# A loop over four experts, six of eleven weight positions and one token operand buffer in a mixture-of-experts kernel

## What is computed

```
g_idx = argmax(x @ w_group + b_group)                   # one group of 8
top_val, top_idx = top_k(expert logits of that group, 2)  # 2 of its 8 experts
h = silu(xb @ w_gate[e]) * (xb @ w_up[e])               # e = 0..63, width 512
y += gate * (h @ w_down[e])
```

## Time and profile before

| what | us |
|---|---|
| median of three executions | 1652.43 |
| the profiled execution: span from first to last instruction | 1650.3 |
| PE busy | 1344.0 |
| ACT busy | 442.9 |
| DVE busy | 539.8 |
| stage of the experts' weights, DMA at full rate, about | 740 to 1637 |

### The profile page before, as it was taken

The page is one execution under the profiler, slowest core; times in us unless marked ns, Lnnn a source line. Parts: engine busy times, 40 slices in busy tenths (PEclk is TensorE's granted clock), DMA queues, the critical chain, the costliest instruction groups (busy, mean ns, idle before and its releaser), DMA issues.

```text
span 1650.3 us, 30064 instructions
## 1 busy us (share of the span) xinstructions
PE 1344.0 (81%) x12966; PEld 1011.0 (61%) x12966; DVE 539.8 (33%) x908; ACT 442.9 (27%) x752; POOL 61.1 (4%) x83
## 2 busy tenths in 40 slices
PE   8999999999999999999667676667667666667655
PEld 8989999878999998876333343343334343334332
DVE  6666555766555578541000000000000000000001
ACT  5354433644433356421111011011011011101101
POOL 3000000001000025000000000000000000000000
PEclk9999999999999999999988987898798798998797
DMA  9545453533555544389999999999999999999996
GB/s 348 193 174 179 177 203 124 180 117 120 201 189 178 179 149 174 153 356 428 428 427 425 428 427 427 426 427 428 427 426 427 427 427 427 427 428 426 427 427 251
DMA packets 45842, 520.37 MB, mean 315 GB/s; under 512 B 5535, under 2 KB 5796, under 8 KB 8228
## 3 DMA queue, kind: packets, MB, share of 16 engines
q1 hardware_dynamic: 44496, 517.12, 76.9%
q0 software_dynamic: 1040, 1.52, 0.4%
q10 hardware_dynamic: 196, 0.08, 0.0%
HBM read 517.65 MB, written 1.05 MB: 314 GB/s over the span
## 4 chain that ended last, share of the span: by engine, by line
DMA 48%; PE 45%; DVE 4%; ACT 2%; issue 1%; POOL 0%; DVEq 0%; SPq 0%; ACTq 0%
DMA ring<-in_moe_units 28%; DMA x_slots<-in_moe_units 14%; PE ps L265 11%; PE ps L267 11%; PE ps L266 11%; DMA work<-in_moe_units 6%; PE ps L2057 4%; PE ps L2066 2%; DVE w_split L230 1%; PE ps L2080 1%; PE ps L2100 1%; PE ps L272 1%; DVE xT_lo L512 1%; ACT w_split L226 0%; PE ps L942 0%
## 5 line engine op out<-in xcount | busy, mean ns | idle before, releaser
L265 PE MATMUL ps<-xT_hi,w_split 128*128 128x256 f32 x960 | 269.7, 281 | 1.8 <-DVE xT_lo L512 1.8
L230 DVE TENSOR_TENSOR w_split<-ring,w_split 128x2048 fp32r<-128x2048 f32 (+2 forms) x105 | 237.2, 2261 | 97.6 <-ACT w_split L226 96.4
L267 PE MATMUL ps<-xT_hi,w_split 128*128 128x256 f32 x960 | 268.2, 279 | 0.0
L266 PE MATMUL ps<-xT_lo,w_split 128*128 128x256 f32 x960 | 268.1, 279 | 0.0
L2258 DVE TENSOR_TENSOR work<-ps,work 128x128 f32<-128x128 f32 x64 | 18.7, 292 | 755.4 <-ACT work L2183 755.4
L2057 PE MATMUL ps<-ring,work 128*32 128x256 f32 x2464 | 182.5, 447 | 95.3 <-DMA ring<-in_moe_units 95.2
L226 ACT ACTIVATE w_split<-ring 128x2048 fp32r<-128x2048 f32 (+2 forms) x109 | 203.7, 1871 | 153.0 <-PE ps L267 153.0
L2057 PEld LDWEIGHTS ps<-ring,work 128*32 128x32 f32 x2464 | 84.6, 124 | 185.3 <-DMA ring<-in_moe_units 101.5
L265 PEld LDWEIGHTS ps<-xT_hi,w_split 128*128 128x128 f32 x960 | 180.2, 188 | 4.0 <-issue 2.9
L266 PEld LDWEIGHTS ps<-xT_lo,w_split 128*128 128x128 f32 x960 | 179.9, 187 | 0.9
L267 PEld LDWEIGHTS ps<-xT_hi,w_split 128*128 128x128 f32 x960 | 180.4, 188 | 0.0
(11 more groups left out here) (341 smaller groups left out, 1665.5 us busy)
## 6 DMA issues: line engine op xcount, KB each, us to landing
ring<-in_moe_units SPq DMA_DIRECT2D x114, 2048.0 KB, 46.7
work<-in_moe_units SPq DMA_DIRECT2D x38, 2048.0 KB, 46.6
x_slots<-in_moe_units SPq DMA_DIRECT2D x38, 2048.0 KB, 46.6
ring<-in_ffn_units SPq DMA_DIRECT2D x66, 1024.0 KB, 4.8
ring<-in_conv_units SPq DMA_DIRECT2D x15, 1024.0 KB, 11.4
ring<-in_win_units SPq DMA_DIRECT2D x9, 1024.0 KB, 4.8
ring<-in_wo_units SPq DMA_DIRECT2D x4, 1024.0 KB, 5.5
ring<-in_wout_units SPq DMA_DIRECT2D x4, 1024.0 KB, 4.8
```

The lines of the kernel that those rows point to most:

```text
L230: dve.tensor_tensor(w_split[:, u % SPLIT, 1, 0:n], raw[:, u % RAW, 0:n], w_split[:, u % SPLIT, 0, 0:n].bitcast(F32), ALU.subtract).then_in ...
L265: pe.matmul(out_ap, stat_hi, mov_hi, start=first, stop=False, skip_group_check=True)
L266: pe.matmul(out_ap, stat_hi, mov_lo, start=False, stop=False, skip_group_check=True)
L267: return pe.matmul(out_ap, stat_lo, mov_hi, start=False, stop=last, skip_group_check=True)
```

## The change

The loop body holds 4 steps in place of 20 and is run 13 times; steps 1 to 9 are written out ahead of it. `kept_slot` becomes an ordinary position, so there are eleven. Doubles 0 to 28 go round all eleven; from double 29 on (`RING_FROM`) the stream goes round six of them (places 7, 8, 9, 10, 0, 1: five pieces of `ring` and one of `x_slots`). SP's loop body holds six doubles and is run 26 times; its issues ahead of that are written out. A double waits for the reading of the one eleven earlier in the first part, six earlier from double 35 on. The token operand has one buffer. ACT therefore writes its first half in the step of lane 3, between `turned` and `gu_out`, in place of lane 2, after `gu_out`.

```diff
-    xstat = [wk(XSTAT + 1024 * b, 1024).rearrange("p (k m) -> p k m", m=P) for b in range(3)]
+    xstat = wk(XSTAT, 1024).rearrange("p (k m) -> p k m", m=P)
...
-    FIRST_STEP, LOOP = 2, 20
-    LOOPS = (NE - FIRST_STEP) // LOOP
+    FIRST_STEP, LOOP = 10, 4
+    LOOPS = (NE - 2 - FIRST_STEP) // LOOP
...
-    SLOTS = 10
+    SLOTS = 11
+    KEPT = 4
     LOOP_DOUBLES = 3 * LOOP
-    KEPT = 4
+    RING_FROM, IN_RING = 3 * FIRST_STEP - 1, 6
...
     def place(d):
 
-        return (d if d < KEPT else d - 1) % SLOTS
+        if d >= RING_FROM:
+            d = RING_FROM + (d - RING_FROM) % IN_RING
+        return d % SLOTS
+
+    def last_in(d):
+
+        return d - (IN_RING if d >= RING_FROM + IN_RING else SLOTS)
...
+        def refill(r, d):
+            sp.wait_ge(s("moe_read"), r * DOUBLES + last_in(d) + 1)
+            whole(d, d)
...
-            for k in range(SLOTS):
-                sp.wait_ge(s("moe_read"), r * DOUBLES + (k + 1 if k < KEPT else k + 2))
-                whole(SLOTS + k + 1, SLOTS + k + 1)
-            with sp.Fori(2, (DOUBLES - 1) // SLOTS) as i:
-                for k in range(SLOTS):
-                    sp.wait_ge(s("moe_read"), r * DOUBLES + i * SLOTS + (k - SLOTS + 2))
-                    whole(SLOTS + k + 1, i * SLOTS + (k + 1))
-            sp.wait_ge(s("moe_read"), r * DOUBLES + (DOUBLES - 1 - SLOTS + 1))
+            for d in range(SLOTS, RING_FROM + IN_RING):
+                refill(r, d)
+            first = RING_FROM + IN_RING
+            with sp.Fori(0, (DOUBLES - 1 - first) // IN_RING) as i:
+                for k in range(IN_RING):
+                    sp.wait_ge(s("moe_read"), r * DOUBLES + i * IN_RING + (last_in(first + k) + 1))
+                    whole(first + k, i * IN_RING + (first + k))
+            sp.wait_ge(s("moe_read"), r * DOUBLES + last_in(DOUBLES - 1) + 1)
...
             turned(E - 1, 1 - par, T_BANK)
+            if more and lane == 3:
+                x_half(quad + 1)
             gu_out(at, d, par)
-            if more and lane == 2:
-                x_half(quad + 1, x_buffer(q // QUAD + 1))
             y_out(at, d + 2, 1 - par, T_BANK)
...
-            one_step(step, r, 1, True)
+            for e in range(1, FIRST_STEP):
+                one_step(step, r, e, True)
```

More of the change, by code:

```diff
@@ L1938, in program @@
     QUADS = NE // QUAD
-    FIRST_STEP, LOOP = 2, 20
-    LOOPS = (NE - FIRST_STEP) // LOOP
+    FIRST_STEP, LOOP = 10, 4
+    LOOPS = (NE - 2 - FIRST_STEP) // LOOP
     DOUBLES = 3 * NE
-    SLOTS = 10
+    SLOTS = 11
+    KEPT = 4
     LOOP_DOUBLES = 3 * LOOP
-    KEPT = 4
-    assert KEPT < 3 * FIRST_STEP - 1
+    RING_FROM, IN_RING = 3 * FIRST_STEP - 1, 6
+    assert LOOPS * LOOP + FIRST_STEP == NE - 2 and LOOP == QUAD
+    assert LOOP_DOUBLES % IN_RING == 0 and RING_FROM > 2 * SLOTS
     def place(d):
-        return (d if d < KEPT else d - 1) % SLOTS
-    assert LOOP_DOUBLES % SLOTS == 0 and LOOP % QUAD == 0 and LOOP // QUAD == 5
-    assert LOOPS * LOOP + FIRST_STEP == NE - 2
+        if d >= RING_FROM:
[3 more added lines that the diff above has]
+        return d - (IN_RING if d >= RING_FROM + IN_RING else SLOTS)
     def expert_loop(eng, r, step):
@@ L1965, in one_step @@
         step(e, r * NE + e, r * QUADS + e // QUAD, e - i * LOOP, more, (r, i))
-    def x_buffer(quad):
-        return xstat[(0, 1, 0, 1, 2)[quad % 5]]
     def slot_of(d):
-        if d == KEPT:
+        if place(d) == KEPT:
             return kept_slot[:, :, :]
-        k = place(d)
+        k = place(d) - (place(d) > KEPT)
         if k in (0, 1, 5):
@@ L1992, in turn_of @@
         k = place(d)
-        return r * len(range(k, DOUBLES - 1, SLOTS)) + i * (LOOP_DOUBLES // SLOTS) + ((d if d < KEPT else d - 1) // SLOTS + 1)
+        every = sum(place(x) == k for x in range(DOUBLES))
+        ringed = k in [place(RING_FROM + x) for x in range(IN_RING)]
+        return r * every + (i * (LOOP_DOUBLES // IN_RING) if ringed else 0) + sum(place(x) == k for x in range(d + 1))
     def doubles_before(at, d):
@@ L2012, in whole @@
         def whole(d, at):
-            sp.dma_start(slot_of(d), a["moe_units"][bass.ds(at, 1)].rearrange("a p (u n) -> p (a u) n", u=2))\
-                .then_inc(s("moe_kept") if d == KEPT else landed(d), 16)
+            sp.dma_start(slot_of(d), a["moe_units"][bass.ds(at, 1)].rearrange("a p (u n) -> p (a u) n", u=2)).then_inc(landed(d), 16)
+        def refill(r, d):
+            sp.wait_ge(s("moe_read"), r * DOUBLES + last_in(d) + 1)
+            whole(d, d)
         def one_round(r):
@@ L2018, in one_round @@
                 sp.wait_ge(s("combined"), r + 1)
-            if isinstance(r, int):
+                for d in range(SLOTS):
+                    whole(d, d)
+            else:
                 whole(KEPT, KEPT)
-            for k in range(SLOTS):
-                if isinstance(r, int):
+                for k in range(SLOTS - 1):
                     first_free(k)
-                whole(k if k < KEPT else k + 1, k if k < KEPT else k + 1)
-            for k in range(SLOTS):
-                sp.wait_ge(s("moe_read"), r * DOUBLES + (k + 1 if k < KEPT else k + 2))
-                whole(SLOTS + k + 1, SLOTS + k + 1)
-            with sp.Fori(2, (DOUBLES - 1) // SLOTS) as i:
-                for k in range(SLOTS):
-                    sp.wait_ge(s("moe_read"), r * DOUBLES + i * SLOTS + (k - SLOTS + 2))
-                    whole(SLOTS + k + 1, i * SLOTS + (k + 1))
-            sp.wait_ge(s("moe_read"), r * DOUBLES + (DOUBLES - 1 - SLOTS + 1))
+                    d = k + (k >= KEPT)
+                    whole(d, d)
+            for d in range(SLOTS, RING_FROM + IN_RING):
[6 more added lines that the diff above has]
+            sp.wait_ge(s("moe_read"), r * DOUBLES + last_in(DOUBLES - 1) + 1)
             for half, sem in ((0, landed(DOUBLES - 1)), (1, s("moe_last"))):
@@ L2045, in double, with up_like @@
         def double(at, d):
[L2046 to L2049, removed]
+            pe.wait_ge(landed(d), turn_of(at, d) * 16)
             return slot_of(d)
-        def up_like(at, d, b, x, lane, half):
+        def up_like(at, d, b, lane, half):
             w = double(at, d).rearrange("p u (k s c) -> p (u k) s c", k=2, s=2)
@@ L2056, in up_like @@
                 for j in range(QUAD):
-                    last = pe.matmul(ps[CAP * j:CAP * j + CAP, b, 0:BLK], x[:, 4 * half + k, CAP * lane:CAP * lane + CAP],
+                    last = pe.matmul(ps[CAP * j:CAP * j + CAP, b, 0:BLK], xstat[:, 4 * half + k, CAP * lane:CAP * lane + CAP],
                                      w[:, k, j // 2, BLK * (j % 2):BLK * (j % 2) + BLK], start=half == k == 0, stop=half == 1 and k == 3,
@@ L2106, in step @@
             d, par, lane = 3 * q - 1, q % 2, q % QUAD
-            x = x_buffer(q // QUAD)
             if lane == 0:
                 pe.wait_ge(s("xa"), quad + 1)
-            up_like(at, d, par, x, lane, 0)
+            up_like(at, d, par, lane, 0)
             pe.wait_ge(s("y_out"), E)
             turn(E - 1, 1 - par, T_BANK)
-            if q >= FIRST_STEP:
+            if q >= 2:
                 combine(par)
@@ L2116, in step @@
                 pe.wait_ge(s("xd"), quad + 1)
-            up_like(at, d + 1, par, x, lane, 1)
+            up_like(at, d + 1, par, lane, 1)
             if more and lane >= 2:
@@ L2129, in one_round @@
             pe.wait_ge(s("xa"), quad + 1)
-            up_like((r, 0), 0, 0, xstat[0], 0, 0)
+            up_like((r, 0), 0, 0, 0, 0)
             pe.wait_ge(s("xd"), quad + 1)
-            up_like((r, 0), 1, 0, xstat[0], 0, 1)
-            one_step(step, r, 1, True)
+            up_like((r, 0), 1, 0, 0, 1)
+            for e in range(1, FIRST_STEP):
+                one_step(step, r, e, True)
             expert_loop(pe, r, step)
@@ L2141, in one_round @@
             d = 3 * q - 1
-            x = x_buffer(q // QUAD)
-            up_like(at, d, 1, x, QUAD - 1, 0)
+            up_like(at, d, 1, QUAD - 1, 0)
             pe.wait_ge(s("y_out"), g + (NE - 1))
@@ L2146, in one_round @@
             combine(1)
-            up_like(at, d + 1, 1, x, QUAD - 1, 1)
+            up_like(at, d + 1, 1, QUAD - 1, 1)
             pe.wait_ge(s("a_mul"), g + (NE - 1))
@@ L2167, in moe_act, with x_half @@
         act.sem_inc(s("y_out"), 1)
-        def x_half(quad, buf):
+        def x_half(quad):
             act.wait_ge(s("x_first"), quad + 1)
             for k in range(4):
-                last = act.activation(buf[:, k, :], bank(X_BANK, P, P * k), ACT.Copy, scale=col("norm2", k))
+                last = act.activation(xstat[:, k, :], bank(X_BANK, P, P * k), ACT.Copy, scale=col("norm2", k))
             last.then_inc(s("xa"), 1)
@@ L2200, in one_round @@
             g = r * NE
-            x_half(r * QUADS, xstat[0])
+            x_half(r * QUADS)
             gu_out((r, 0), 0, 0)
-            one_step(step, r, 1, True)
+            for e in range(1, FIRST_STEP):
+                one_step(step, r, e, True)
             expert_loop(act, r, step)
```

(8 more changed lines are left out.)

## The result

The changed kernel takes 1642.07 us (median of four, 1640.07 to 1646.30), the kernel before 1653.56 us (four, 1652.24 to 1656.77). The ratio is 0.993, interval 0.9913 to 0.9947: faster by 0.7%, 11.5 us. The prediction said no change, 1652.4, and the time lies outside its range.

A forecast was written before the change was run, and what follows sets the result against it. The weights' DMA stream was taken to bound the kernel: 737.2 + 901.0 + 12.1 = 1650.3 us span, all changes 0, plus 2.1 to the median gave 1652.4 us, range 1648.5 to 1658.

The forecast's parts named there:

- What bounds the kernel: Experts' stage: it lasts as long as its bytes take, 4.89 us a double at 427 GB/s, PE busy 68%.
- Start of the stream: First refill: eleven positions are filled ahead in both kernels and it still waits for double 0's reading; effect 0.
- Six positions in place of ten: DMA queue from double 35 on: issue to landing falls to 27.1 us in the median, 15.6 us slack left; cost 0.
- The bound of 2 us for another rate: Stream with the shorter queue: same rate taken; 427 against 428 GB/s, 0.2%, gives 2 us on either side.
- Ten more turns: Loop jumps of PE, ACT and DVE, 12 for 2: PE catches up after each; cost 0, 49 us if uncovered.
- Rival (a): PE's 12 jumps: fetch stalls add up beyond 15.6 us and idle DMA, giving 1676 to 1701 us; chance 0.03.
- The fetches' use of the DMA engines: Instruction packets in the stream, priced by bytes at 427 GB/s: 0 taken, ends -1.5 and +0.9 us.
- The rest of the sum: Stream from first refill to last landing: some 13 us of 901 in doubles longer than 4.89 us, cause not read.
- Rival (c): Stream: the 13 us of longer doubles hang on positions or long queues and go, down to 1640 us; chance 0.05.
- One token operand: ACT's first half in lane 3: written 1.2 to 2.5 us before PE comes to its wait; cost 0.
- The tail: ACT's idle time before the closing squares, with a jump over a shorter copy: up to 1.2 us shorter or unchanged; taken 0.

The follow-up runs named there:

- the run with 9000 increments: The changed kernel with 9000 semaphore increments, which nothing waits for, on idle GpSimd during the experts' stage: 1689.33 us, ratio 1.0216.
- the longer copy: The changed kernel with 600 instructions more on ScalarE in the second, unrun copy of the rounds' code, jumped over before the closing squares: 1642.98 us, ratio 0.9932.

## Why the prediction was wrong, by its steps

- What bounds the kernel: right. The stage is the stream's in all twelve kernels, and whatever left the stream alone left the time alone.
- Start of the stream, 0: right as far as can be seen; its position varies by 6 us between executions.
- Six positions in place of ten, cost 0 with 15.6 us of slack: right, and shown with three positions. The bound of 2 us for another rate was not needed.
- Ten more turns, cost 0 on the path: right in the sum, wrong in what happens. The stalls of 5 us do not multiply, they vanish, since the short loop needs no fetch after its first pass. Rival (a), stalls that add up, had none to add.
- **The fetches' use of the DMA engines is the step that failed.** It read "if the loop of four steps stayed in the engine's store, some 40 packets would go, 1.5 us less", and took 0. The mechanism was named, 50 packets went, and they were worth 9.5 us. The price had been worked out from bytes, spread over all sixteen engines at the whole rate. But a packet holds up one engine, and the stream waits for the most delayed one: 1.46 us for each round of PE's packets over eight engines. From a loop of 20 against a loop of 4 each of PE's packets is worth 0.20 us of stream (9.6 us for 48), from 38 experts written out 0.24, and each of GpSimd's, all on one engine, 0.65.
- The rest of the sum, "some 13 us are left, doubles that took longer than 4.89, whose cause I do not read from these rows": most of it, 9.5 us, was the same quantity; 3.4 are left in the changed kernel (891.5 - 885.1 - 3). Two things of the same stretch, a price by bytes of 2 us and an unexplained rest of 13 us, should have been laid beside each other. Rival (c) let the rest go with the positions or the queue, and gave it 0.05; the loop of twenty on the new positions shows that it is neither. Its argument against, "every slice has them alike", could not tell: a slice of 41 us does not resolve one late double in 117 us, and the rate of all engines does not show a late one, as the run with 9000 increments has it.
- One token operand, 0: right, ratio 0.9995.
- The tail, "up to 1.2 us shorter, or stay", taken 0: it was 1.2, of which the longer copy gave back 0.9 in the profile. By the count that gives 23 written steps before, the second copy has 15 now and not 16.

In all: -9.5 for the stream and -1.2 for the tail, where the sum had 0 and 0.

What stays open: the records of DMA packets carry no number of the engine, so that PE's packets use eight and GpSimd's one is read from the shares at the end of the stream and from the period of the long doubles. A 16 KB packet is recorded with 1.0 to 1.1 us and makes a double 1.46 late, an 8 KB packet with 0.31 and 0.65; what the rest goes to is not shown. Nor is it shown why 2021 instructions do not stay. The stream of the loop of eight is 1 to 2 us longer than 55 packets at 0.19 or 0.20 us make it.

## What to carry to other kernels

Where a stage runs at the full rate of the DMA engines, count its instruction packets: a body short enough to stay in the engine's store (here 1012 instructions of TensorE, not 2021) gives back more than their bytes say, and an engine that executes long written-out code beside the stream takes it away, even if nothing waits for that engine. Read the pace of the landings and the last microseconds of the stream, where the late engines work alone; the mean rate hides an engine that is late. Price such a load by the DMA engine that it falls on, not by its share of all sixteen. And when a sum leaves a rest of some us that recurs at a regular distance, find what else recurs at that distance before calling an edit free.

## What the runs showed of the hardware that was not expected

- A loop of TensorE of 1012 instructions ran 13 times with no instruction packet after its first pass; one of 2021 was fetched anew on each turn, with waits of up to 5.5 us on issue.
- 70 packets of 8 KB for GpSimd's instructions, 0.2% of the DMA engines' time by the queues' table, lengthened a stream of 891 us by 45.8 us, 5%, and 35 of them by 20.8 us.
- TensorE's instruction packets go round eight of the sixteen DMA engines (DMA share 0.51 and 0.48 from 1625 to 1635 us, near the end of the stream, a long double once in eight packets), GpSimd's fall on one (share 0.06 at the end). A stream at full rate then ends with the late engines working alone.
- Beside those 70, 48 more packets of TensorE's cost nothing, though alone they cost 9.6 us.
- Three positions of 2 MB, issue to landing 12.4 us, carry the stream as fast as six with 27.1 us (891.4 and 891.5 us).
